# Heads of a latent attention beside their keys and values, and norm squares added on GpSimd

## What is computed

```python
def rms_norm_2(x, g):
    xf = x.astype(jnp.float32)
    y = xf * lax.rsqrt(jnp.mean(xf * xf, axis=-1, keepdims=True) + RMS_EPS)
    return (y * g.astype(jnp.float32)).astype(x.dtype)

    # mla_branch: 16 heads, 128 + 64 dimensions of key, 128 of value
    q = (rms_norm_2(c_q, q_norm) @ w_uq).reshape(B, S, N_HEADS, QK_HEAD_DIM)
    kv = (rms_norm_2(c_kv, kv_norm) @ w_ukv).reshape(B, S, N_HEADS, QK_NOPE_DIM + V_HEAD_DIM)
    k_nope, v = kv[..., :QK_NOPE_DIM], kv[..., QK_NOPE_DIM:]
    s = (jnp.einsum('bqhd,bkhd->bhqk', qn, k_nope) + jnp.einsum('bqhd,bkd->bhqk', qp, k_pe))
    prob = jax.nn.softmax(jnp.where(causal, s * scale, -jnp.inf), axis=-1)
    o = jnp.einsum('bhqk,bkhd->bqhd', prob, v)
    return o.reshape(B, S, N_HEADS * V_HEAD_DIM) @ w_attn_o
```

## Time and profile before

| | us |
|---|---|
| median of 3 runs | 3984.12 (3983.2 to 3996.94) |
| the profiled execution | 3994.0 |
| its span | 3992.2 |
| TensorE busy | 3401.6 |
| VectorE busy | 2475.8 |
| ScalarE busy | 1387.5 |
| GpSimd busy | 738.4 |
| mean granted clock of TensorE | 0.92 |

### The profile page before, as it was taken

How to read it: one execution, slowest core, us unless ns; L and a number is a source line. 1 busy time by engine, 2 the same in 40 slices (tenths; PEclk the granted TensorE clock), 3 DMA queues, 4 the chain that set the end, 5 groups by cost and what they waited for, 6 DMA issues and landing times.

```text
span 3992.2 us, 53452 instructions
## 1 busy us (share of the span) xinstructions
PE 3401.6 (85%) x21298; PEld 2802.1 (70%) x21298; DVE 2475.8 (62%) x3304; ACT 1387.5 (35%) x1972; POOL 738.4 (18%) x516
## 2 busy tenths in 40 slices
PE   8999888999999999899999997766666766666688
PEld 7888778999999999899998797742222223222248
DVE  5667765654455456754554555977777777555555
ACT  4345444653344444544444443220110001100133
POOL 0000000000000000000000000235565665565620
PEclk9999889999999999999998898887888888878899
DMA  6443234456555565456454254889999999999964
GB/s 216 127 127 108 89 109 130 157 182 190 181 179 189 174 197 165 136 173 183 152 181 126 75 182 144 334 319 422 422 422 422 422 421 417 422 420 422 422 261 132
DMA packets 187593, 953.17 MB, mean 239 GB/s; under 512 B 20817, under 2 KB 21073, under 8 KB 121425
## 3 DMA queue, kind: packets, MB, share of 16 engines
q0 software_dynamic: 73728, 536.90, 32.7%
q1 hardware_dynamic: 112464, 407.68, 32.3%
q10 hardware_dynamic: 1152, 5.17, 0.3%
HBM read 947.58 MB, written 2.10 MB: 238 GB/s over the span
## 4 chain that ended last, share of the span: by engine, by line
PE 63%; DMA 17%; DVE 10%; POOL 4%; ACT 3%; issue 2%; DVEq 0%; ACTq 0%; SPq 0%; POOLq 0%
PE ps L441 63%; DMA BIG<-in_peer_v,CS 8%; DMA HLF<-in_peer_v,CS 5%; DVE HL L1492 2%; DMA HF<-in_peer_v,CS 2%; POOL HLF L429 2%; POOL BIG L429 1%; DVE BIG L1496 1%; DMA HLF<-in_peer_u,CS 1%; DVE BIG L2035 1%; DVE BIG L1492 1%; DMA BIG<-in_peer_u,CS 1%; PE ps L445 1%; DVE TMP L1496 1%; ACT HS L973 0%
## 5 line engine op out<-in xcount | busy, mean ns | idle before, releaser
L441 PE MATMUL ps<-HS,HL 128*128 128x256 f32 x11936 | 1531.8, 288 | 68.1 <-DVE HL L1492 51.1
L441 PEld LDWEIGHTS ps<-HS,HL 128*128 128x128 f32 x11936 | 1496.2, 196 | 83.2 <-DVE HL L1492 55.2
L1492 DVE TENSOR_TENSOR HL<-RAW,HL 128x1024 fp32r<-128x1024 f32 (+1 forms) x772 | 939.6, 1217 | 217.9 <-ACT HL L977 155.3
L977 ACT CAST HL<-RAW 128x1024 fp32r<-128x1024 f32 (+1 forms) x772 | 805.6, 1044 | 646.7 <-PE ps L441 602.3
L441 PE MATMUL ps<-BIGR,HL 128*128 128x256 f32 x5680 | 746.0, 285 | 1.5 <-DVE BIGR L1492 1.5
L441 PEld LDWEIGHTS ps<-BIGR,HL 128*128 128x128 f32 x5680 | 708.7, 192 | 7.8 <-issue 3.7
L429 POOL DMA_INDIRECT BIG<-in_peer_u,CS x133 | 182.5, 1372 | 2726.6 <-DVE CS L1500 2499.6
L441 PE MATMUL ps<-BIG,HF 128*128 128x512 f32 (+1 forms) x760 | 404.7, 683 | 183.9 <-DMA BIG<-in_peer_v,CS 160.3
L441 PE MATMUL ps<-HLF,HF 128*128 128x512 f32 x656 | 349.8, 687 | 152.5 <-DMA HLF<-in_peer_v,CS 139.3
L441 PEld LDWEIGHTS ps<-BIG,HF 128*128 128x128 f32 (+1 forms) x760 | 163.7, 226 | 419.9 <-issue 386.9
L2035 DVE CUSTOM_DVE_ANT_0 BIG<-BIG 128x2048 f32<-128x2048 f32 x133 | 304.9, 2293 | 165.4 <-DMA BIG<-in_peer_u,CS 156.5
(11 more groups left out here) (170 smaller groups left out, 2181.6 us busy)
## 6 DMA issues: line engine op xcount, KB each, us to landing
RAW<-in_w_up SPq DMA_DIRECT2D x128, 512.0 KB, 4.0
RAW<-in_w_down SPq DMA_DIRECT2D x128, 512.0 KB, 4.2
RAW<-in_w_out SPq DMA_DIRECT2D x64, 512.0 KB, 3.7
RAW<-in_w_qk SPq DMA_DIRECT2D x32, 512.0 KB, 4.4
RAW<-in_w_xbc SPq DMA_DIRECT2D x32, 512.0 KB, 3.6
RAW<-in_w_xr SPq DMA_DIRECT2D x32, 512.0 KB, 3.8
RAW<-in_w_yr SPq DMA_DIRECT2D x32, 512.0 KB, 3.9
RAW<-in_w_gr SPq DMA_DIRECT2D x32, 512.0 KB, 4.0
```

What stands on the lines that cost most here:

```text
L441: return e.matmul(o, l, r, start=start, stop=stop, skip_group_check=True)
L977: s.done(e.copy(o, i), sig)
L1492: v.done(e.tensor_tensor(o, a, b, op), sig)
```

## The change

1. `w2_uk` and `w2_uv` become sixteen layers of one unit, `w2_uk0`, `w2_uv0`, `w2_uk1`, ... A key unit is followed by the rope of one pair of queries. Behind each unit but the first one step of the heads' pipeline runs, so head h starts when its keys and those before are there; the last three steps run in `w2_ao`.
2. The output of a head is split as it leaves PSUM: ScalarE's copy writes the high half, VectorE subtracts it from the bank for the low half, and this subtraction frees the bank. The split behind the last head goes.
3. In `w2_ao` the first six units are taken in another order: the first halves of chunks 0 to 2, then their second halves.
4. For g_mix, g_cross, g_mlp, attn_norm, ffn_norm and the final norm GpSimd adds the squares in SBUF (NSUM) and TensorE multiplies the sum once by the ones, in `norm_end`. The other norms stay.

```diff
+UKV = [(f"w2_u{x}{i}", 2, 4, 256, 1, x == "v") for i in range(8) for x in "kv"]
-          ("w2_uk", 16, 4, 256, 1, False), ("w2_uv", 16, 4, 256, 1, True), ("w2_ao", 16, 8, 128, 2, False),
+          *UKV, ("w2_ao", 16, 8, 128, 2, False),
+        self.order = [(b, p) for b in range(self.blocks) for p in range(self.parts)]
+        if self.name in LATE:
+            self.order[:6] = [(b, p) for p in range(2) for b in range(3)]
...
         def gpsimd(e):
+            def square_sums(name, m):
+                for c in range(0, 16, m):
+                    q = PSQ[name] + c // m + 1
+                    sq = sq_slot(c, m)
+                    g.wait_ge(s_psq, q)
+                    for j in range(m):
+                        sig = (s_padd, q) if j == m - 1 else None
+                        g.prev()
+                        if c + j == 0:
+                            g.done(e.tensor_copy(NSUM[:, :], sq[:, 0, :]), sig)
+                        else:
+                            g.done(e.tensor_tensor(NSUM[:, :], NSUM[:, :], sq[:, j, :], ALU.add), sig)
+            square_sums("g_mix", 4)
+            for name in ("g_cross", "g_mlp", "attn_norm", "ffn_norm"):
+                square_sums(name, 1)
...
+            square_sums("final", 1)
...
             def norm_end(name):
-                for c in range(13, 16):
-                    norm_sum(name, c)
+                pe.wait_ge(s_padd, PSQ[name] + (4 if name == "g_mix" else 16))
+                pe.wait_ge(s_nfree, NORM[name])
+                mm(norm_bank[:, 0:T], con("ones"), NSUM[:, :], True, True).then_inc(s_nsum, 1)
...
-            dense(L["w_out"], mixed, residual("g_cross"), g_ck)
+            dense(L["w_out"], mixed, None, g_ck)
...
-            drain(pipeline(mla(h) for h in range(16)))
-            dense(L["w2_ao"], cut_by(hs, s_os, lambda k: k // 4 + 1))
+            g_ml = pipeline(mla(h) for h in range(16))
+            for i in range(8):
+                dense(L[f"w2_uk{i}"], low)
+                bank_done(L["w2_uq"], 16 + i)
+                rope2(SCORE["mla"] + MLAS[i], QP[:, i, :])
+                if i:
+                    step(g_ml)
+                dense(L[f"w2_uv{i}"], low, None, g_ml)
+            step(g_ml)
+            dense(L["w2_ao"], cut_by(os_, s_ofree, lambda k: OUTS["mla"] + k + 1), None, g_ml)
...
+            def squared(name, c, m=1):
+                q = PSQ[name] + c // m + 1
+                if c >= 8:
+                    s.wait_ge(s_padd, q - 8 // m)
+                act(sq_slot(c, m), X[:, c:c + m, :], ACT.Square, (s_psq, q))
...
-                copy(o, out_bank[lo:lo + rows, 0:T], (s_ofree, OUTS[name] + h + 1))
+                copy(o, out_bank[lo:lo + rows, 0:T], (s_ohi, h + 1) if name == "mla" else (s_ofree, OUTS[name] + h + 1))
...
-            for c in range(0, 16, 4):
-                copy(hs[0][:, c:c + 4, :], QN[:, c:c + 4, :], (s_ohi, c // 4 + 1))
...
-                for _ in range(ahead + 1):
-                    yield
+                for _ in range(ahead):
+                    yield
+                if name == "mla":
+                    v.wait_ge(s_ohi, h + 1)
+                    tt(os_[1][:, h, :], out_bank[:, 0:T], os_[0][:, h, :].bitcast(F32), ALU.subtract,
+                       (s_ofree, OUTS["mla"] + h + 1))
+                yield
```

More of the change, by code:

```diff
@@ L69, in done @@
         b, j = divmod(c, self.per)
-        return self.after(self.unit0 + (b + 1) * self.parts - 1, j)
+        return self.after(self.unit0 + self.order.index((b, self.parts - 1)), j)
     def end(self):
@@ L98 @@
 OUTS = counted([("attn", 16), ("ssd", 16), ("cross", 4), ("mla", 16)])
-SQ = counted([("g_mix", 4), ("mem", 4), ("attn", 2), ("ssm", 4), ("g_cross", 16),
-              ("g_mlp", 16), ("attn_norm", 16), ("q_norm", 2), ("kv_norm", 1), ("ffn_norm", 16), ("ple_norm", 8),
-              ("final", 16)])
+SQ = counted([("mem", 4), ("attn", 2), ("ssm", 4), ("q_norm", 2), ("kv_norm", 1), ("ple_norm", 8)])
+PSQ = counted([("g_mix", 4), ("g_cross", 16), ("g_mlp", 16), ("attn_norm", 16), ("ffn_norm", 16), ("final", 16)])
+ADDED = counted([(n, 1) for n in ("g_mix", "g_cross", "g_mlp", "attn_norm", "ffn_norm", "final")])
 HSQ = counted([("rope", 4), ("ck", 1), ("cq", 1)])
@@ L173, in build @@
         L, NUNITS = stream()
-        STREAM = [A[n][i] for n, a in L.items() for i in range(a.units)]
+        STREAM = [A[n[:5]][int(n[5:])] if n[:5] in ("w2_uk", "w2_uv") else A[n][b * a.parts + p]
+                  for n, a in L.items() for b, p in a.order]
         X = sb("X", [128, 16, T])
@@ L455, in dense @@
                 for u in range(L.unit0, L.unit0 + L.units):
-                    block, part = divmod(u - L.unit0, L.parts)
+                    block, part = L.order[u - L.unit0]
                     pe.wait_ge(s_lo, u + 1)
@@ L718, in tensor @@
             pe.wait_ge(s_vec, 16)
-            for j in range(4):
-                norm_sum("g_mix", j, 4)
+            norm_end("g_mix")
             g_an = angles()
@@ L766, in tensor @@
             drain(pipeline(cross(h) for h in range(4)))
-            dense(L["w_co"], cut_by(cx, s_cx, lambda k: k + 1), residual("g_mlp"))
+            dense(L["w_co"], cut_by(cx, s_cx, lambda k: k + 1))
             norm_end("g_mlp")
@@ L770, in tensor @@
                 dense(L[f"w_up{half}"], normed("g_mlp"))
-                dense(L[f"w_down{half}"], cut_by(hid, s_hid, lambda k: 32 * half + k + 1),
-                      residual("attn_norm") if half else None)
+                dense(L[f"w_down{half}"], cut_by(hid, s_hid, lambda k: 32 * half + k + 1))
             norm_end("attn_norm")
@@ L949, in tensor @@
             half_sum(1, 3)
[L951 to L959, removed]
+            dense(L["w2_pg"], cut_by(hg, s_nlo, lambda k: NORMED["ple_norm"] + k + 1))
+            norm_end("final")
         @block.scalar
```

120 lines of the change are left out of this document (59 added, 61 removed).

## The result

| | before | after |
|---|---|---|
| median, us | 3983.96 (3982.57 to 3996.94, 5 runs) | 3959.33 (3954.25 to 3961.72, 5 runs) |
| profiled execution, us | 3994.0 | 3960.17 |
| its span, us | 3992.2 | 3958.4 |

The ratio of the medians is 0.9928, 95% interval [0.9913, 0.9943]: 24.6 us less. Between the two profiled executions it is 33.8 us. The forecast was 3942 with a range of 3930 to 3964, so the time lies inside the range but 17.3 us above the forecast, close to the exclusion rival's 3956.

The account below looks back on a forecast made before the run. TensorE was taken to set the pace up to 2485 us, then DMA, then TensorE again. -28.4 - 12.0 - 0.3 - 4.9 + 1.6 + 2.0 = -42.0 us took 3994.0 to 3952.0 profiled, 3942 as median; range 3930 to 3964.

Parts of the forecast that it names:

- exclusion rival: GpSimd's adds and VectorE's two-SBUF-operand work exclude each other, at the start and in w_co: 14.6 us, 3956, 30%.
- Part 1, the heads: Latent attention's heads run beside key and value units: from 143.3 to 114.9 us, a gain of 28.4.
- A step of 3.07 + 3.50 = 6.57 us: Interleaved attention stage: one weight unit 3.07 plus heads' parts 3.50 on TensorE; sixteen steps make 105.1 us.
- The cover of the new wait: VectorE waits for ScalarE's copy of head h-3; TensorE wants the probabilities queued behind one unit, 3 us, later.
- The terms for w2_ao: First chunk of w2_ao at full clock 5.8 us, plus 0.6 of switches for three steps run in it.
- Norms in the full layers: g_cross, attn_norm, ffn_norm: each saves 5.0 us of TensorE stream and pays 1.0 at its end; together -12.0.
- The final norm: Fourteen sums inside the last projection leave TensorE at 0.42 us each, 1.0 paid at the end: -4.9 us.
- g_mlp: the step that failed first: In w_co VectorE and ScalarE would set the period, 3.56 for 3.72 us: 1.3 gained, 1.0 paid, -0.3.
- g_mix: right in kind, low in size: At the kernel's start, four adds, handovers and one product delay the first dense matmul: +1.6 us.
- Clock, +2.0: Longer idle waits at the six new norm ends may cost TensorE clock: +2.0 us, between 0 and 9.
- From 3952 to 3942: Whole kernel: the profiled execution's saving carried to the median of three runs, 9.9 us lower.
- The other rivals: Sums worth nothing, 3963, 6%; interleaved attention steps in series, about 4042, 4%; cheaper adds, no clock loss, 3936, 10%.

Follow-up runs that it names:

- the kernel with the heads alone: The changed kernel with all six norms summed on TensorE as before, only the latent attention changed: 3965.89 us, ratio 0.993 to the kernel before.
- the memset: The changed kernel, but for g_mlp GpSimd sets NSUM to one instead of adding each square, waits kept, sum left out: 3953.94 us in one run.
- the copy: The changed kernel, but for g_mlp GpSimd copies each square into NSUM instead of adding it, waits kept, sum left out: 3954.34 us in one run.

## Why the prediction was right, and where it wasn't

**Part 1, the heads: right, in the steps and in the total.** A step of 3.07 + 3.50 = 6.57 us: measured 6.78 and 6.37, mean 6.57, with half a rope in it; the ropes, put at 0.42, were 0.44. VectorE's 4.5 us of work in 6.57 is 47.04 of 70 measured, 4.4. The cover of the new wait held in all steps but one at the end (1.75 us). -28.4 was forecast, -28.3 came as the whole of the kernel with the heads alone and -26.9 in its stage. Both are taken against runs of the kernel before that have the long stretch of low clock, as the forecast was. The terms for w2_ao, 5.8 and 0.6, weren't read apart.

**Norms in the full layers: right.** Chunks every 5.76 us, as forecast. The add is 0.72 us alone. The estimate by the Trainium skill, GPSIMD Engine Reference, section "Elementwise — side-by-side cycle accounting", was 0.6. Counted from the last addition to X, the end of g_cross came 2.33 - 1.53 = 0.80 us later, for the 1.0 taken. With g_mlp undone, w_out to w2_low takes 961.8 us against 967.9: -6.1 where g_cross, attn_norm's layer and an untouched g_mlp make -9.0. ffn_norm's stage shows 357.4 against 363.8 without it, -6.4, for -4.0. The final norm and all behind the first gather: -5.9 for -4.9. What the first lacks the other two make up.

**g_mlp: the step that failed first.** The forecast wrote that with the sums gone VectorE and ScalarE set w_co's period at 3.56 us, and -0.3 came of it. It was 4.60 where VectorE sets it, and the norm cost 8.5 us. The exclusion rival had the mechanism and the price of a unit, 1.04, but charged it eight times, 8.3 us. The first four and a half units showed no wait. VectorE's additions to X, from the second to the last, spread over 29.83 us (707.32 to 737.15), and over 25.26 with the memset (707.97 to 733.23): 4.6 us for the exclusion. They spread over the same 25.26 in the kernel before (706.10 to 731.36), so taking the sums off TensorE gave nothing here, where the forecast had 1.3. What is left of the 8.5 is the longer wait at the end, 5.84 us of idle time where the kernel before had 0.32, and the half clock behind it. That the rival's 8.3 comes so near 8.5 is luck.

The Trainium skill (SBUF — State Buffer, section "Who interferes with whom") says that a VectorE instruction with two SBUF inputs and a GpSimd instruction that reads SBUF exclude each other. The rows agree in kind: 0.49 against 0.93 and 1.23 against 1.82 with the add, the copy itself stretched from 0.40 to 1.15, and nothing stretched with the memset, which reads nothing. What VectorE lost, 0.45 and 0.59 us, is somewhat less than the 0.65 to 0.73 that the add beside it still had to run. I gave this 30% and kept 47% for a sum without it, on the ground that no row showed GpSimd computing. That no row shows a thing was no evidence against it, while VectorE's 3.04 us in 3.56 said that w_co had no room for any.

**g_mix: right in kind, low in size.** +1.6 was taken, +2.65 measured at the first dense matmul (29.53 - 26.88), +3.7 between two kernels. The add was taken at 0.6 us, and the twelve of the start took 10.52, 0.88 each, beside VectorE's operations; the upper bound of +5 had adds of 1.4.

**Clock, +2.0.** Three of the new ends were followed by half clock: 6.8 us with g_mlp's 5.84 us of idle time, of which some 2.3 fall into the idle time itself, and 3.4 us each after attn_norm (behind its second wait, 2.30 us) and right behind ffn_norm's 2.36. Half of the busy part is lost at most, 2.3 + 2 x 1.7 = 5.7 us where +2.0 was charged, of which 2.3 is in g_mlp's 8.5. At most, because a later wait can give a part back, as the rows of attn_norm above show.

**From 3952 to 3942: the step that cost most.** The sum of -42.0 was made in the profiled execution, at 3994.0, and came out as -33.8. Against that gap of 8.2 stand 8.8 for g_mlp and 2.1 for g_mix, so all else came out 2.7 better, which is within what two executions of one kernel differ by. Then "the same saving gives 3942 as the new median" took it over to 3984.1. That holds if two executions differ by something that the change leaves alone. Here, as far as the runs show, they differ by the very thing that it removes: 12 to 14 us lost to low clock in the old heads. The profiled execution, in which I read the 6.52 us a head, has them; the one that gave the median 3984.1 is of the lower group, which by the inference above has not. The changed kernel has one group, so the median lost only 24.6. Of the 17.3 us by which the forecast missed, 9.2 are this step and 8.2 the sum. The spread of the three runs shown (3983 and 3997, nothing between) and the clock of 0.70 were both there to be put together. The forecast's other near hit, the exclusion rival's 3956 beside 3959.33, is in part luck too: g_mlp and g_mix missed by 10.9 us together where it charged 14.6, and the 9.2 us of this step, which it did not foresee, lie on top.

**The other rivals.** No step came near 9.2 us; heads and sums did not run in series. The sums were worth what the two periods said.

## What to carry to other kernels

Before an elementwise step goes to GpSimd, look at whether VectorE runs two-operand SBUF work beside it: where VectorE had slack (w_out, a chunk every 5.76 us as forecast) it was free, and where VectorE set the pace (the last units of w_co) each pair cost 0.45 to 0.59 us beside an add of 0.73. When a sum of parts moves off TensorE, give it all parts but the last few, and let TensorE take those in the time in which it waits anyway. And when a kernel's runs fall into two groups, work out which group the profile is from and whether the change removes what parts them, before a saving is taken from one to the other.

## What the runs showed of the hardware

- GpSimd adds 128x256 f32 in 0.72 us and copies it in 0.40 when nothing is beside it; beside VectorE's operations on two SBUF operands an add took up to 1.8 us and a copy 1.15. VectorE's operation on one SBUF and one PSUM operand stayed at 0.42 us beside either.
- The same wait of 2.56 us, in the same code, was followed by 37 to 41 us at 1.2 GHz in three executions and by 10 in another kernel's. Once down, the clock stayed down through heads in which TensorE was 94% busy (58.4 of 62 us). What decides between the two wasn't found.
- Eight products that nobody reads, in a wait of 2.56 us, took 15 us off the stage, and none of twelve runs was in the upper group of times, where seven of seventeen had been.
